# Modulation product of each DeltaNet head: from sixteen accumulating TensorE matmuls to partial products on GpSimd and four matmuls with ones

## The chip, the cores and the metric

The kernel runs on one core of a Trainium2 chip. The metric is the device time of one execution in microseconds (us), the median of several runs. A core has TensorE (matmuls, results in PSUM), VectorE, ScalarE and GpSimd (elementwise work), and SyncE, whose queue issues nearly all of the transfers here. The profiles call them PE (PEld for its weight loads), DVE, ACT, POOL and SP.

## What is computed

One layer of a hybrid backbone, over 512 latent and 128 context tokens of width 1024. What matters here is the modulation, and that DeltaNet runs head by head:

```python
m = jax.nn.silu(cond) @ w_ada + b_ada      # 1024 -> 6144, for cond = c and cond = c_ctx
sh1, sc1, g1, sh2, sc2, g2 = jnp.split(m, 6, axis=-1)
h = modulate(x, norm1_g, sh1, sc1)          # the first third of m is needed at once
qkv, z, bl, al, na, gt = split_in(h, w_in)
o_dn = deltanet_branch(...)                 # 8 heads, each with a triangular solve per chunk
x = x + g1 * merge(...)                     # the other two thirds are needed from here on
x = x + g2 * swiglu(modulate(x, norm2_g, sh2, sc2), ...)
```

## The kernel before

The first 2048 columns of `w_ada` are multiplied at the start. The other 4096 are spread over the eight DeltaNet heads, 512 columns a head in two halves of 256 (`PAIR`). A half of the weights, 8 row blocks of 128 x 256, is loaded into `WA`, one buffer for both halves: the queue of SyncE issues the first half in `opening` (L984), the second in `ada_second` (L988) once the first has been read. TensorE makes a half with `ada_rows` (L1285): eight matmuls, one for each row block k, with the two columns of `csT` (SiLU of the two conditions) as weights, spread over four column groups j = k % 4 of the array, so that four partial sums stand in rows 32j of bank 4. ScalarE copies them to `arow` ("ada half", L2265, and "ada rows", L2280), and `rows_out` (L993) stores them to rows 32j + 2h of `heads_rows`. In the last head, matmuls with a selecting matrix (L1656) add the four partial sums of all heads and turn them, and ScalarE copies them to `mods`.

The order on each engine is written out by hand. A `Steps` object counts the named steps of an engine, and others wait for a step's value. In a head TensorE interleaves two things. One is the DeltaNet head itself: block products P4, Y4, P5, Y5 (`wide`, L1553) and their turns (L1559), P6, Y6 (L1593, L1600), then a scan of five steps. The other is the dense projection of the next strips (L1311, six matmuls per step k), handed out by `filler(fill, n)`; the table `before` says how many steps stand in front of which block product, twelve in front of P4:

```python
for n in (4, 5):
    filler(fill, before[f"P{n}"])
    wait(dve_dn, f"X{n - 1}")
```

X3, which P4 waits for, is made by VectorE. Its chain begins with the ten products of L2909, goes on with transposes and shuffles (L2919 to L2931), then 15 pairs of "term" (L2945) and "lane" (L2947), each waiting for the one before it, and ends with L2954. Among them stand splits of the weights into a rounded part and a rest (`small`, L2903), `vrow` (L2936, L2937), and later the copies of P6 and Y6 (L2988, L2991).

GpSimd has three instructions in a head: the product "A" (L3569), which waits for X3 and which the scan needs, and the two sums of the decays (L3556, L3559).

Of the kernel before, what the change touches and what calls it, by code (L numbers as in the profile page):

```python
# [14 lines left out]
P = 128  # L15
# [98 lines left out]
def pe_steps():  # L114
    names = ["turn k v"]
    for n in (4, 5):
        names += [f"P{n} wide"] + (["ada half"] if n == 4 else []) + [f"P{n}", f"Y{n} wide"] + (["ada rows"] if n == 5 else []) + [f"Y{n}"]
    names += ["P6", "Y6"]
    for s in range(NT):
        if s:  # L120
            names += [f"ks {s} {d}" for d in "fb"]
        names += [f"y {s} {d}" for d in "fb"]
        names += [f"av {s} {d}" for d in "fb"]
    return names + ["norm", "kq", "turn o"]


def act_steps():
    names = ["kq", "L32", "L diag", "hi 1", "hi 2", "L pairs", "kd", "hi 2 late", "P4", "hi 3", "ada half", "Y4", "hi 4", "P5 wide", "P5", "Y5 wide", "Y5", "ada rows", "hi 5", "P6", "hi z", "decay", "Y6"]
# [140 lines left out]
POOL_STEPS = ["A", "dt"]  # L269
# [154 lines left out]
def build(nc, A):  # L424
    top = ExitStack()
    with top:
# [227 lines left out]
        sb("under_vrow", [P, 2 * 136 * U - 120 * U], dn)  # L654
        all_rows = sb("all_rows", [P, 120 * U], dn)[:, :]
# [8 lines left out]
        ob = sb("ob", [P, 2, NT, P], dn)  # L664
        prm = sb("prm", [P, NPRM, U], dn)
# [246 lines left out]
        def _(e):  # L912
# [59 lines left out]
            def opening(h, decays_of_next):  # L972
# [27 lines left out]
            def head(h, strips_after_next):  # L1000
# [12 lines left out]
                rows_out(h)  # L1013
# [9 lines left out]
                extra_store(h, 2)  # L1023

# [78 lines left out]
            rows_out(last)  # L1103
# [11 lines left out]
            pa_in(1)  # L1115
            e.wait_ge(st_e, 16 * (NE * (H - 1) + NE_LAST - 1) + 16)
# [139 lines left out]
        def _(e):  # L1256
# [202 lines left out]
            def head(h, part):  # L1459
# [58 lines left out]
                def filler(queue, n):  # L1518
# [9 lines left out]
                    "first": (12, 0, 3, 1, 1, 1, 1, 0, 2, 1, 1, 1),  # L1528
                    "mid": (12, 2, 2, 2, 2, 2, 2, 1, 3, 2, 1, 1),
# [9 lines left out]
                wait(act_dn, "silu v", h - 1)  # L1539
                for w in range(2):  # L1540
# [21 lines left out]
                for n in (4, 5):  # L1562
# [74 lines left out]

                def turn_o():
# [26 lines left out]
                if not more:  # L1665
# [366 lines left out]
        def _(e):  # L2032
# [167 lines left out]
            def head(h, part):  # L2200
# [4 lines left out]

                def big(at):
# [56 lines left out]
                wait(pe_dn, "ada half")  # L2263
                e.wait_ge(rows_kept, h * 4 * 16)
                act_dn.done(e.activation(arow[:, 0:2 * P], ps[:, 4, 0:2 * P], ACT.Copy), "ada half")  # L2265
# [13 lines left out]
                wait(pe_dn, "ada rows")  # L2279
                act_dn.done(e.activation(arow[:, 2 * P:4 * P], ps[:, 4, 0:2 * P], ACT.Copy), "ada rows")  # L2280
# [58 lines left out]
                if not more:  # L2339
                    e.wait_ge(ld_f0, 48)  # L2340
                    wait(pool_dn, "A")
                    act_na.done(e.activation(sq0, f0[:, 0:2, :], ACT.Square), "sq 0")
                    e.wait_ge(mods_mm, 1)
# [12 lines left out]
                if more:  # L2356
                    norm(h)
                    products_out(h + 1)
# [338 lines left out]
        def _(e):  # L2697
# [389 lines left out]
            e.wait_ge(pe_dn.sem, pe_dn.value(H - 1, "ada rows"))  # L3087
# [118 lines left out]
            e.wait_ge(mods_out, 1)  # L3206
# [329 lines left out]
        def _(e):  # L3536
# [12 lines left out]
            pool_dn.leave_out("dt")  # L3549
            pool_dn.settle(e)  # L3550
# [9 lines left out]

            def head(h, more):
                def wait(steps, name, turn=h):
                    e.wait_ge(steps.sem, steps.value(turn, name))

                wait(dve_dn, "X3")
# [8 lines left out]
                else:  # L3574
                    pool_dn.pass_to("A")

            for h in range(H - 1):
# [80 lines left out]
```

## Time and profile before

| | |
|---|---|
| median of 3 runs | 1302.97 us (1302.94 to 1303.77) |
| the profiled execution | 1302.37 us, its span 1300.6 us |
| TensorE busy | 1284.3 us, 99% |
| VectorE busy | 962.6 us, 74% |
| ScalarE busy | 701.2 us, 54% |
| GpSimd busy | 172.8 us, 13% |
| a middle head of DeltaNet | 74 us (282 to 356, for one) |

Busy is time in which an instruction of the engine runs. Matmuls overlap each other, so a busy TensorE need not be at its peak, and what an instruction costs there is read from the distance between starts. Times in the rows below count from the span's start.

### The profile page before, as it was taken

The numbers are of one execution on the slowest core, as the hardware profiler recorded it, in microseconds if no ns is written. First come the engines' busy times: TensorE is split into PE (matmuls) and PEld (weight loads), VectorE is DVE, ScalarE is ACT, GpSimd is POOL, SyncE is SP. The second block draws the span as 40 slices with busy tenths as digits, with TensorE's granted clock in tenths as the row PEclk, the third lists the DMA queues.
The fourth block names the chain that finished last, engine by engine and source line by source line (L and its number), as shares of the span: only waits on it lengthen the run. The fifth ranks groups of instructions, "written<-read, shape, count | busy, mean of one in ns | idle before, by whom it ended". The sixth has DMA issues, their size and how long they took to land.

```text
span 1300.6 us, 26090 instructions
## 1 busy us (share of the span) xinstructions
PE 1284.3 (99%) x9814; PEld 1212.4 (93%) x9814; DVE 962.6 (74%) x2396; ACT 701.2 (54%) x1578; POOL 172.8 (13%) x161
## 2 busy tenths in 40 slices
PE   7999999999999999999999999999999999999998
PEld 6898999999999999999988889999999999999998
DVE  6677867667686867767456666668999698987995
ACT  5564746465564746465366664347564355634643
POOL 1002020202001020200302320000103300041022
PEclk9999999999999999999999999999999999999999
DMA  9743543434243334325335216431323323233313
GB/s 313 242 131 96 166 122 100 118 94 118 55 142 90 116 103 120 89 72 153 115 113 169 77 51 207 124 82 33 98 67 97 98 70 93 66 100 96 83 57 106
DMA packets 207715, 144.51 MB, mean 111 GB/s; under 512 B 9455, under 2 KB 197015, under 8 KB 207463
## 3 DMA queue, kind: packets, MB, share of 16 engines
q1 hardware_dynamic: 207303, 142.72, 37.4%
q8 instruction: 78, 1.28, 0.4%
q14 instruction: 46, 0.38, 0.1%
q10 hardware_dynamic: 288, 0.13, 0.0%
HBM read 126.67 MB, written 17.99 MB: 111 GB/s over the span
## 4 chain that ended last, share of the span: by engine, by line
PE 92%; DVE 3%; SPq 2%; ACT 1%; issue 1%; DMA 1%; DVEq 0%; ACTq 0%
PE ps L1311 32%; PE ps L1957 25%; PE ps L1700 7%; PE ps L1615 3%; PE ps L1841 2%; PE ps L1937 2%; PE ps L1553 2%; PE ps L1622 2%; SPq L931 2%; PE ps L1439 1%; PE ps L1634 1%; PE ps L1809 1%; PE ps L1285 1%; PE ps L1795 1%; PE ps L1916 1%; PE ps L1693 1%
## 5 line engine op out<-in xcount | busy, mean ns | idle before, releaser
L1311 PE MATMUL ps<-hT_r,WAH_r 128*128 128x320 f32 x624 | 154.9, 329 | 0.5
L1311 PE MATMUL ps<-xT_r,WAH_r 128*128 128x320 f32 x624 | 142.0, 309 | 0.0
L1957 PE MATMUL ps<-d_part_r,W_r 128*128 128x320 f32 x660 | 136.7, 310 | 1.1 <-DVE xT L3388 0.7
L1311 PE MATMUL ps<-hT_r,W_r 128*128 128x320 f32 x588 | 132.6, 308 | 0.0
L1311 PEld LDWEIGHTS ps<-hT_r,WAH_r 128*128 128x128 f32 x624 | 100.3, 189 | 10.8 <-issue 9.8
L1957 PEld LDWEIGHTS ps<-d_part_r,W_r 128*128 128x128 f32 x660 | 107.5, 188 | 2.0 <-DVE xT L3388 1.3
L1957 PE MATMUL ps<-t_big_r,W_r 128*128 128x320 f32 x380 | 107.6, 311 | 0.7 <-ACT naT L2576 0.4
L1311 PEld LDWEIGHTS ps<-xT_r,WAH_r 128*128 128x128 f32 x624 | 104.5, 188 | 0.0
L1957 PE MATMUL ps<-b_part,W_r 128*128 128x320 f32 x456 | 101.2, 309 | 0.0
L1311 PEld LDWEIGHTS ps<-hT_r,W_r 128*128 128x128 f32 x588 | 97.9, 188 | 0.1
L1957 PE MATMUL ps<-t_small_r,W_r 128*128 128x320 f32 x304 | 93.9, 309 | 0.0
L1311 PE MATMUL ps<-hT_r,naT_r 128*128 128x320 f32 x398 | 90.9, 309 | 0.5 <-DVE xT_r L2753 0.4
L3569 POOL TENSOR_TENSOR gm<-sqkq,dt 128x1280 f32<-128x1280 f32 x8 | 23.5, 2938 | 500.6 <-DVE Xc L2954 500.6
L1957 PEld LDWEIGHTS ps<-b_part,W_r 128*128 128x128 f32 x456 | 76.2, 188 | 0.0
L3623 POOL TENSOR_TENSOR oT<-oT 128x512 f32<-128x512 f32 (+1 forms) x12 | 19.9, 1658 | 408.7 <-PE ps L1957 280.0
L1311 PE MATMUL ps<-hT_r,WH_more 128*128 128x320 f32 x286 | 70.8, 329 | 0.3
L1957 PEld LDWEIGHTS ps<-t_big_r,W_r 128*128 128x128 f32 x380 | 69.0, 188 | 2.1 <-ACT naT L2576 1.5
L1311 PEld LDWEIGHTS ps<-hT_r,naT_r 128*128 128x128 f32 x398 | 66.2, 188 | 4.0 <-DVE xT_r L2753 3.1
L3388 DVE SCALAR_TENSOR_TENSOR xT<-ps,mods,xT 128x192 f32<-128x192 f32 (+2 forms) x132 | 51.0, 421 | 20.5 <-PE ps L1957 19.9
L2518 ACT ACTIVATE W_r<-oT 128x512 fp32r<-128x512 f32 (+1 forms) x101 | 61.0, 607 | 7.3 <-PE ps L1957 7.3
L1311 PE MATMUL ps<-xT_r,WH_more 128*128 128x320 f32 x286 | 64.9, 308 | 0.0
L1957 PEld LDWEIGHTS ps<-t_small_r,W_r 128*128 128x128 f32 x304 | 57.1, 188 | 0.0
(489 smaller groups left out, 3426.7 us busy)
## 6 DMA issues: line engine op xcount, KB each, us to landing
oT<-in_ffn_w SPq DMA_DIRECT2D x44, 512.0 KB, 5.2
W<-in_w_in SPq DMA_DIRECT2D x36, 512.0 KB, 4.5
WAH<-in_w_ada SPq DMA_DIRECT2D x16, 1024.0 KB, 7.1
naT<-in_w_in SPq DMA_DIRECT2D x24, 512.0 KB, 4.2
ext_dram<-naT SPq DMA_DIRECT2D x28, 320.0 KB, 4.2
oT<-in_ffn_w SPq DMA_DIRECT2D x32, 256.0 KB, 3.9
tA<-ext_dram SPq DMA_DIRECT2D x16, 320.0 KB, 3.7
GCB<-gc_dram SPq DMA_DIRECT2D x7, 640.0 KB, 4.6
```

The costliest lines, as they stand in the source:

```text
L931: e.dma_start(WP[i][:, 4 * j:4 * j + 4, kind * PAIR:(kind + 1) * PAIR], src).then_inc(ld_wp[i][j], 16)
L1311: m = e.matmul(ps[:, bank + b, 0:n], w[:, k, :], x[:, k, a:a + n], start=k == 0 and i == 0, stop=k == KD - 1 and i == 2, skip_group_check= ...
L1553: m = e.matmul(ps[g:g + 32, 5, r:r + P], one[:, u, :], other[:, u, :], start=True, stop=True, skip_group_check=True)
L1615: m = e.matmul(ps[:, 2 + d, w * P:(w + 1) * P], kq[:, tile[d], w, :], S[:, d, :], start=True, stop=True, skip_group_check=True)
L1622: m = e.matmul(ps[:, (4, 6)[d], 0:P], XT[:, u, :], rr[:, d, :] if s else vrow[:, CT, :], start=True, stop=True)
L1700: m = e.matmul(ps[:, bank + b, 0:n], w[:, k, :], x[:, k, a:a + n], start=k == 0 and i == 0, stop=k == k_n - 1 and i == 2, skip_group_check ...
L1841: m = e.matmul(ps[:, PB_BANKS[n % 3] + b, 0:c], w, x[:, a:a + c], start=k == 0 and i == 0, stop=k == KP - 1 and i == 2, skip_group_check=True)
L1937: m = e.matmul(ps[:, UP_BANKS[p][s] + b, 0:HT], w[i][:, k % 4, :], operand(xp, k, b), start=k == 0 and n == 0, stop=k == KD - 1 and n == 2 ...
L1957: m = e.matmul(ps[:, bank, 0:HT], w[i][:, k, :], x[i][:, k, :], start=start and k == 0 and j == 0, stop=k == half - 1 and j == 2, skip_gro ...
L2518: act_ff.done(e.activation(w_big[i][:, 0:tiles_half(p), :], raw_half(p, s, j), ACT.Copy), f"{o} {p}")
L3388: m = e.scalar_tensor_tensor(x, ps[:, bank, a - half * HT:a - half * HT + w], mods[:, 2 * g + s + 40, c:c + 1], x, ALU.mult, ALU.add)
L3569: pool_dn.done(e.tensor_tensor(typed(AT[:, :, :]), kqs[:, :, 1, :].unsqueeze(1).to_broadcast([P, 2, NT, P]), typed(dtm[:, :, :]), ALU.mult ...
```

## The change

The eight row blocks of a half are no longer multiplied by TensorE. GpSimd scales each block with the two columns of `csT` (per row of the block, that is per partition) and adds up the eight results: 16 `tensor_scalar` of 128x256 and 7 `tensor_tensor` of 128x512 a half. The first half stands in front of "A", the second behind the decay sums. What is left is one sum over the 128 partitions for each condition and half. TensorE makes it at the head's end with four matmuls with ones, and ScalarE evacuates all with one copy. `WA` is free for the next load when GpSimd has read it. The stores to `heads_rows` are single rows now, at the end of the head's part of the queue; in the last head they stand behind the load of the second `w_pa` strip. In TensorE's order the filler steps of the gaps in which the halves stood are shared out anew; in the middle heads one moves from in front of P6 to in front of the turn of Y5.

```diff
-POOL_STEPS = ["A", "dt"]
+POOL_STEPS = ada_names(0) + ["A", "dt"] + ada_names(1)
...
-                e.wait_ge(pe_dn.sem, pe_dn.value(h - 1, "ada rows"))
+                e.wait_ge(pool_dn.sem, pool_dn.value(h - 1, "plus 1 7"))
                 e.dma_start(WA, w_ada[:, :, ds((16 + h * 4) * P, 2 * P)]).then_inc(ld_wa[0], 16)
...
-                e.wait_ge(pe_dn.sem, pe_dn.value(h, "ada half"))
+                e.wait_ge(pool_dn.sem, pool_dn.value(h, "plus 0 7"))
                 e.dma_start(WA, w_ada[:, :, ds((18 + h * 4) * P, 2 * P)]).then_inc(ld_wa[1], 16)
...
             def rows_out(h):
-                e.wait_ge(act_dn.sem, act_dn.value(h, "ada rows"))
+                e.wait_ge(mods_out, h + 1)
                 for j in range(4):
-                    e.dma_start(heads_rows[32 * j + 2 * h:32 * j + 2 * h + 2, :], arow[32 * j:32 * j + 2, :]).then_inc(rows_kept, 16)
+                    v, half = j // 2, j % 2
+                    row = 32 * half + 2 * h + v
+                    e.dma_start(heads_rows[row:row + 1, half * PAIR:(half + 1) * PAIR], arow[32 * j:32 * j + 1, 0:PAIR]).then_inc(rows_kept, 16)
...
-                    "first": (12, 0, 3, 1, 1, 1, 1, 0, 2, 1, 1, 1),
-                    "mid": (12, 2, 2, 2, 2, 2, 2, 1, 3, 2, 1, 1),
+                    "first": (12, 1, 2, 1, 1, 1, 1, 1, 1, 1, 1, 1),
+                    "mid": (12, 2, 2, 2, 2, 2, 2, 2, 2, 2, 1, 1),
...
-                    if n == 4:
-                        wait(act_dn, "kd")
-                        pe_dn.done(ada_rows(4, 2 * P, WA, ld_wa[0:1], h * 16 + 16), "ada half")
...
-                    if n == 5:
-                        wait(act_dn, "ada half")
-                        pe_dn.done(ada_rows(4, 2 * P, WA, ld_wa[1:2], h * 16 + 16), "ada rows")
...
+                def ada_of_head():
+
+                    wait(pool_dn, "plus 1 7")
+                    wait(act_dn, f"v {NT - 1} b")
+                    for j in range(4):
+                        m = e.matmul(ps[32 * j:32 * j + 32, 4, 0:PAIR], ONES[:, 0:32], ada_sums[:, j % 2, j // 2, :], start=True, stop=True, skip_group_check=True)
+                    m.then_inc(mods_mm, 1)
...
                         norm_rows()
+                        ada_of_head()
+                    if not more and k == 0:
+                        ada_of_head()
                     if not more and k == KD // 2:
                         e.wait_ge(rows_kept, H * 4 * 16)
...
+                def ada_rows_out():
+
+                    e.wait_ge(mods_mm, h + 1)
+                    if h:
+                        e.wait_ge(rows_kept, h * 4 * 16)
+                    e.activation(arow[:, 0:PAIR], ps[:, 4, 0:PAIR], ACT.Copy).then_inc(mods_out, 1)
...
+            def ada_half(h, half):
+
+                e.wait_ge(ld_wa[half], h * 16 + 16)
+                if h and not half:
+                    e.wait_ge(mods_mm, h)
+                total = ada_sums[:, half, :, :]
+
+                def times(k):
+
+                    out = ada_parts[:, k % 3, :, :] if k else total
+                    if k > 3:
+                        e.wait_ge(pool_dn.sem, pool_dn.value(h, f"plus {half} {k - 3}"))
+                    elif 0 < k and (h or half):
+                        e.wait_ge(pool_dn.sem, pool_dn.value(h - 1 + half, f"plus {1 - half} {(6, 7, 5)[k % 3]}"))
+                    for v in range(2):
+                        m = e.tensor_scalar(out[:, v, :], WA[:, k, :], csT[:, k, v:v + 1], None, ALU.mult)
+                    pool_dn.done(m, f"times {half} {k}")
+
+                times(0)
+                times(1)
+                for k in range(1, KD):
+                    if k + 1 < KD:
+                        times(k + 1)
+                    e.wait_ge(pool_dn.sem, pool_dn.value(h, f"plus {half} {k - 1}" if k > 1 else f"times {half} 1"))
+                    pool_dn.done(e.tensor_tensor(total, total, ada_parts[:, k % 3, :, :], ALU.add), f"plus {half} {k}")
...
             def head(h, more):
...
+                ada_half(h, 0)
                 wait(dve_dn, "X3")
...
+                ada_half(h, 1)
```

To make room, `all_rows`, the solve's shuffled rows, moves into `ob`, which is free then.

## Rows read from the trace of the kernel before

**Rows 1.** The page: busy time, TensorE's granted clock in 40 slices, last chain by engine.
```profile
PE 1284.3 (99%) x9814; PEld 1212.4 (93%) x9814; DVE 962.6 (74%) x2396; ACT 701.2 (54%) x1578; POOL 172.8 (13%) x161
...
PEclk9999999999999999999999999999999999999999
...
PE 92%; DVE 3%; SPq 2%; ACT 1%; issue 1%; DMA 1%; DVEq 0%; ACTq 0%
```
**Rows 2.** Timeline, TensorE, 312 to 324: start, duration, line, instructions.
```profile
312.33 0.74 PE L1553 MATMUL ps<-tri,Xc 128*32 128x128 f32 x18
...
313.98 0.57 PE L1311 MATMUL ps<-hT_r,WAH_r 128*128 128x320 f32 x2
...
322.85 0.85 PE L1553 MATMUL ps<-tri,Xc 128*32 128x128 f32 x20
323.63 0.56 PE L1311 MATMUL ps<-hT_r,WH_more 128*128 128x320 f32 x2
```
**Rows 3.** What ended TensorE's idle time before L1553: us in all, times.
```profile
  DVE Xc L2954: 1.4, 7
```
**Rows 4.** Timeline, VectorE, 292 to 313.
```profile
292.57 2.71 DVE L2909 SCALAR_TENSOR_TENSOR tri<-sqkq,bk,dt 128x128 f32<-128x128 f32 x10
...
300.25 1.21 DVE L2903 TENSOR_TENSOR naT_r<-naT,WAH_r 128x1024 fp32r<-128x1024 f32 x1
301.38 0.68 DVE L2936 TENSOR_TENSOR vrow<-ps,nrm 128x512 f32<-128x512 f32 x1
...
302.24 0.31 DVE L2945 TENSOR_TENSOR P6c<-P6c,all_rows 128x150 f32<-128x150 f32 x1
...
311.65 0.49 DVE L2954 TENSOR_TENSOR Xc<-P6c,lv_c 128x320 f32<-128x320 f32 x1
```
**Rows 5.** Groups of instructions, GpSimd, by shape: busy us, mean ns, idle before.
```profile
L3626 POOL TENSOR_TENSOR naT<-oT 128x512 f32<-128x512 f32 x9 | 12.0, 1330 | 2.4 <-PE ps L1957 1.5 <-POOL oT L3623 0.4
...
L3626 POOL TENSOR_TENSOR naT<-oT 128x384 f32<-128x384 f32 x3 | 3.0, 1012 | 0.4
...
L3541 POOL MEMSET X<- 128x320 f32 x1 | 0.4, 366 | 0.0
```
**Rows 6.** Timeline of the feed-forward part, VectorE and GpSimd, 883 to 1001.
```profile
883.91 0.49 DVE L3312 TENSOR_TENSOR b_part<-t_big,b_part 128x320 fp32r<-128x320 f32 x1 [0.33 <-ACT d_part_r L2564]
883.99 1.56 POOL L3623 TENSOR_TENSOR oT<-oT 128x512 f32<-128x512 f32 x1 [128.64 <-DMA oT<-in_ffn_w]
884.32 1.58 DVE L3312 TENSOR_TENSOR d_part_r<-t_big,d_part_r 128x320 fp32r<-128x320 f32 x1
...
997.15 0.68 DVE L3246 TENSOR_TENSOR W_r<-oT,W_r 128x512 fp32r<-128x512 f32 x1
997.47 2.12 POOL L3623 TENSOR_TENSOR oT<-oT 128x512 f32<-128x512 f32 x1 [3.52 <-PE ps L1957]
997.75 0.68 DVE L3246 TENSOR_TENSOR oT_r<-oT,W_r 128x512 fp32r<-128x512 f32 x1
...
999.74 1.30 POOL L3626 TENSOR_TENSOR naT<-oT 128x512 f32<-128x512 f32 x1
1000.86 0.55 DVE L3388 SCALAR_TENSOR_TENSOR xT<-ps,mods,xT 128x320 f32<-128x320 f32 x1 [1.08 <-PE ps L1957]
```
**Rows 7.** The first half's load in the window 282 to 290: issue and landing.
```profile
L984 SPq DMA_DIRECT2D WAH<-in_w_ada x1: 581/581/581, 282.8 to 282.8; - x1
...
DMA to landing us min/median/max: 8.7/8.7/8.7
```
**Rows 8.** Timeline, 320 to 337: GpSimd, VectorE, TensorE.
```profile
320.54 2.94 POOL L3559 TENSOR_TENSOR dt<-dt,msk 128x1280 f32<-128x1280 f32 x1
...
334.53 0.48 DVE L2988 COPY P6c<-ps 64x320 f32<-64x320 f32 x1
...
336.05 0.80 PE L1600 MATMUL ps<-XT,P6c 64*64 64x64 f32 x20
```
**Rows 9.** Timeline, SyncE's queue, 625 to 640: the last head's row stores.
```profile
634.79 2.45 SPq L993 DMA_DIRECT2D heads_rows<-arow  x4
```
**Rows 10.** Transfers by line: count, KB each, median us from issue to landing.
```profile
S<-in_state_dn SPq DMA_DIRECT2D x16, 64.0 KB, 1.9
```

More of the change, by code:

```diff
@@ L116, in pe_steps @@
     for n in (4, 5):
-        names += [f"P{n} wide"] + (["ada half"] if n == 4 else []) + [f"P{n}", f"Y{n} wide"] + (["ada rows"] if n == 5 else []) + [f"Y{n}"]
+        names += [f"P{n} wide", f"P{n}", f"Y{n} wide", f"Y{n}"]
     names += ["P6", "Y6"]
@@ L127, in act_steps @@
 def act_steps():
-    names = ["kq", "L32", "L diag", "hi 1", "hi 2", "L pairs", "kd", "hi 2 late", "P4", "hi 3", "ada half", "Y4", "hi 4", "P5 wide", "P5", "Y5 wide", "Y5", "ada rows", "hi 5", "P6", "hi z", "decay", "Y6"]
+    names = ["kq", "L32", "L diag", "hi 1", "hi 2", "L pairs", "kd", "hi 2 late", "P4", "hi 3", "Y4", "hi 4", "P5 wide", "P5", "Y5 wide", "Y5", "hi 5", "P6", "hi z", "decay", "Y6"]
     for s in range(NT):
@@ L266, in dve_na_steps, with ada_names @@
     return names
-POOL_STEPS = ["A", "dt"]
+def ada_names(half):
+    names = [f"times {half} 0", f"times {half} 1"]
+    for k in range(1, KD):
+        names += [f"times {half} {k + 1}"] if k + 1 < KD else []
+        names += [f"plus {half} {k}"]
+    return names
+POOL_STEPS = ada_names(0) + ["A", "dt"] + ada_names(1)
 OPERANDS = ("A11", "S1", "S2", "A12", "S3", "S4", "A22")
@@ L653, in build @@
         sqkq = sb("sqkq", [P, NT, 2, P], dn)
-        sb("under_vrow", [P, 2 * 136 * U - 120 * U], dn)
-        all_rows = sb("all_rows", [P, 120 * U], dn)[:, :]
+        ada_sums = sb("ada_sums", [P, 2, 2, PAIR], dn)
+        ada_parts = sb("ada_parts", [P, 3, 2, PAIR], dn)
+        sb("under_vrow", [P, 2 * 136 * U - 10 * PAIR], dn)
         vrow = sb("vrow", [P, NT, P], dn)
@@ L664, in build @@
         ob = sb("ob", [P, 2, NT, P], dn)
+        all_rows = ob[:, :, :, :].rearrange("p a t c -> p (a t c)")[:, 0:120 * U]
         prm = sb("prm", [P, NPRM, U], dn)
@@ L1012, in head @@
                 extra_store(h, 1)
-                rows_out(h)
                 if strips_after_next:
@@ L1023, in head @@
                 extra_store(h, 2)
+                rows_out(h)
             e.wait_ge(rows_zero, 1)
@@ L1102, in _ @@
             extra_store(last, 4)
-            rows_out(last)
             e.wait_ge(pe_dn.sem, pe_dn.value(last, "Y6"))
@@ L1115, in _ @@
             pa_in(1)
+            rows_out(last)
             e.wait_ge(st_e, 16 * (NE * (H - 1) + NE_LAST - 1) + 16)
@@ L1539, in head @@
                 wait(act_dn, "silu v", h - 1)
+                if h:
+                    e.wait_ge(mods_out, h)
                 for w in range(2):
@@ L1673, in head @@
                         pe_na.done(m, f"sums {'qk'[j]} 0")
+                    e.wait_ge(mods_out, H)
                     for j in range(2):
@@ L2262, in head @@
                 big("3")
-                wait(pe_dn, "ada half")
-                e.wait_ge(rows_kept, h * 4 * 16)
-                act_dn.done(e.activation(arow[:, 0:2 * P], ps[:, 4, 0:2 * P], ACT.Copy), "ada half")
                 if part != "first":
@@ L2278, in head @@
                 act_dn.done(e.activation(Yc[:, :, :], ps[:, 6, 0:U * 32].rearrange("p (u c) -> p u c", u=U), ACT.Copy), "Y5")
-                wait(pe_dn, "ada rows")
-                act_dn.done(e.activation(arow[:, 2 * P:4 * P], ps[:, 4, 0:2 * P], ACT.Copy), "ada rows")
                 big("5")
@@ L2357, in head @@
                     norm(h)
+                    ada_rows_out()
                     products_out(h + 1)
@@ L3086, in _ @@
             e.wait_ge(gain_q, 1)
-            e.wait_ge(pe_dn.sem, pe_dn.value(H - 1, "ada rows"))
+            e.wait_ge(pool_dn.sem, pool_dn.value(H - 1, "plus 1 7"))
             scaled_q(0, ss0)
@@ L3549, in _ @@
             pool_dn.leave_out("dt")
+            pool_dn.pass_to("times 0 0")
             pool_dn.settle(e)
@@ L3559, in decays @@
                 pool_dn.done(e.tensor_tensor(typed(dt[:, :, :]), typed(dt[:, :, :]), upto, ALU.add), "dt")
+            def ada_half(h, half):
[14 more added lines that the diff above has]
+                times(1)
+                for k in range(1, KD):
+                    if k + 1 < KD:
+                        times(k + 1)
+                    e.wait_ge(pool_dn.sem, pool_dn.value(h, f"plus {half} {k - 1}" if k > 1 else f"times {half} 1"))
+                    pool_dn.done(e.tensor_tensor(total, total, ada_parts[:, k % 3, :, :], ALU.add), f"plus {half} {k}")
             def head(h, more):
@@ L3574, in head @@
                 else:
-                    pool_dn.pass_to("A")
+                    pool_dn.leave_out("dt")
+                ada_half(h, 1)
+            e.wait_ge(cond_silu, 1)
             for h in range(H - 1):
```

6 lines of the change are left out of this document (4 added, 2 removed).

## Prediction

> **What bounds the kernel now.** I read the page first. TensorE is busy in 99% of the span and makes up 92% of the chain that ended last; its clock digit is 9 in every slice [rows 1]. So what leaves TensorE is gained, as long as nothing else makes it wait. The second view was TensorE's timeline in a middle head of DeltaNet, around the two places where the modulation product stands. After the block product P4 (L1553) TensorE runs the half product (L1285) before the next dense matmul (L1311); after P5 it goes straight on [rows 2]. The third view was what TensorE waits for at L1553: in seven of the eight heads it stands 0.2 us for VectorE's L2954, the instruction that makes X3 [rows 3]. That small wait matters most: TensorE has used up its twelve filler steps just as VectorE ends its solve. There is no slack in front of P4, and a VectorE that comes later by d makes TensorE stand still for d. The fourth view was VectorE's own timeline in that stretch. From L2909 at 292.57 to the end of L2954 at 312.14 it has hardly a gap [rows 4]; 30 small products and sums (L2945, L2947) fill most of the time from 302.24 on, each waiting for the one before.
>
> **What the change takes from TensorE.** From P4's start to the next dense matmul 1.65 us pass with the half product in between, 0.78 us at P5 without it [rows 2]. So a half costs 0.87 us, two halves in eight heads 13.9 us. Added at each head's end are four matmuls of the size of the eight that make a half: half of 0.87 is 0.44 us, and I take 0.5 with the switch in front, 4.0 us in all (bounds 3.5 and 6). The filler steps moved between the gaps are the same number. The two evacuations on ScalarE become one; it sits idle around both places, and I price them at nothing.
>
> **What it gives GpSimd.** Each half is 16 scaled copies of 128x256 and seven sums of 128x512. A sum of 128x512 takes 1.33 us in its group (1.30 undisturbed) and one of 128x384 takes 1.01 [rows 5, 6]. The trace has no GpSimd instruction with one tensor and a scalar. Below it lies a memset of 320 elements, 0.37 us, above it a two-input sum of 256 elements, which the two sizes give as 1.33 - 0.32 = about 0.70 us [rows 5]. One input and one output is nearer to the memset; I take 0.35 (bounds 0.31 and 0.70). A half is then 16 x 0.35 + 7 x 1.30 = 14.7 us. The Trainium skill (GPSIMD Engine Reference, Engine selection) calls one-input elementwise work roughly line-rate and two-input work about twice as slow as VectorE; by that the copy would be near 0.3 us and this forecast some 4 us smaller. Two halves are 29.4 us of a head of 74 us, in which GpSimd has had three instructions of 2 to 3 us, so it is not itself the bound.
>
> **When it runs.** The first half's weights are issued at 282.77 and land 8.7 us later, at 291.5 [rows 7]. GpSimd starts there and works through 14.7 us of its own time, just over VectorE's solve, which begins at 292.57.
>
> **What that costs VectorE.** The two engines get in each other's way, and the trace shows it. At 884.32 VectorE starts L3312, otherwise 0.49 us, while GpSimd runs a sum from 883.99 to 885.55: it takes 1.58 us, that is it is held for about 1.1 us, until 0.13 us before GpSimd ends [rows 6]. It goes the other way too: GpSimd's sum at 997.47 takes 2.12 in place of 1.30 us because two VectorE instructions without a wait between them run first. VectorE's L3388, which takes one tensor from PSUM, keeps its normal 0.55 us beside GpSimd [rows 6]. The held ones have both tensors in SBUF. In before's DeltaNet stage GpSimd's three instructions happen to stand beside transposes and such, so nobody is held.
>
> In the solve, L2909, L2903, L2945, L2947 and L2954 have both tensors in SBUF. I walk through one head. Until 292.6 GpSimd does 1.1 of its 14.7 us. L2909 waits for the rest of one instruction, 0.3, then holds GpSimd for 2.7 us. From 295.3 to 300.25 VectorE mostly transposes and shuffles with one input; GpSimd gets 5.0 us done and, with the copies and L2923, delays VectorE by 0.8. L2903 waits 0.5, and beside L2936 and its neighbour, which read PSUM, GpSimd does 0.95. So it has 14.7 - 1.1 - 0.3 - 5.8 - 0.5 - 0.95 = 6.05 us left when the chain of 30 starts. There they take turns. Two copies and a sum are 2.0 us: the sum holds VectorE 1.1 us as above, a copy, mostly hidden in VectorE's own gaps, 0.15. Three such turns make 4.2 us. VectorE is late by 0.3 + 0.8 + 0.5 + 4.2 = 5.8 us at L2954, and TensorE waits as long. Heads 0 and 7 have the load at slightly other times; I count them alike: 8 x 5.8 = 46.4 us. If the copies cost 0.70, a half is 20.3 us, the 5.6 more fall into the chain, copies hold 0.5 each, and the delay is 1.6 + 11.65 x 2.1 / 2.7 = 10.7 us per head, 39 more. If VectorE's chain keeps GpSimd out although it waits between its instructions, only the 1.6 us are left, 33.6 less.
>
> **The second half** starts when GpSimd ends the decay sums, 323.5 [rows 8], and lasts to about 340. VectorE has idle time there, but a weight split (L2903) stands in front of the copy L2988 at 334.53, which TensorE's Y6 at 336.05 waits for [rows 8], and one filler step fewer now stands in front of P6. I take 0.7 us per head, 5.6 in all (bounds 0 and 12).
>
> **The end of the last head.** Before, the row stores left at 634.79 [rows 9], long before the last strip. Now they can leave only after the four matmuls at the last strip's step 0, and TensorE wants them four steps, about 3.5 us, later. They need 0.5 (matmuls), 0.6 (evacuation), 2.45 (the four issues) and a landing; small state loads land in 1.9 us [rows 10]. That is 5.5 us: a stall of about 2 us, once (bounds 0 and 5).
>
> **The sum.** -13.9 + 4.0 + 46.4 + 5.6 + 2.0 = +44.1 us. The profiled execution took 1302.37 us (span 1300.6 and 1.8 around it), 0.6 under the median of 1302.97, so the forecast is 1302.4 + 44.1 = 1346.5 us, 3.4% slower.
>
> **Rivals.**
> (a) Faster. GpSimd's work does not reach the chain in front of P4: its instructions wait, not VectorE's, and they have until the scan, behind Y6, to finish. Then -13.9 + 4.0 + 2.0 = -7.9, 1294.5 us. It decides if VectorE's delay per head stays under (13.9 - 4.0 - 2.0) / 8 = 1.0 us. For it speaks that GpSimd was also held in the trace; against it that L3312 was held 1.10 us by a single sum [rows 6], and seven of them stand in a half.
> (b) VectorE keeps the port in its chain but pays around it: 1.6 us per head. -13.9 + 4.0 + 12.8 + 5.6 + 2.0 = +10.5, 1313 us. Against it: a wait between two instructions leaves a gap, and GpSimd's instruction is already pending.
> (c) The clock falls. In before TensorE never pauses in the heads for more than a few tenths of a us and is granted full speed throughout [rows 1]. A pause of 5.8 us in each head is new. If behind each one TensorE runs at 1.2 GHz for as long as it paused, it loses half of 5.8 us, 2.9 per head: 1346.5 + 23 = 1369.5 us. No row here prices it. The Trainium skill (TensorE: Matmul & The Clock Gate, Rules for kernel authors) warns that idle gaps between bursts of matmuls bring the clock back to the lower level; by that this rival would hold.
>
> **Chances.** The forecast as worked out 0.70, with its own range 1318 to 1380 from the bounds of the copy and of the chain; (a) 0.12; (b) 0.08; (c) 0.10. A range of 1306 to 1375 leaves out (a) and the far end of the slow copies, together under 0.2. A measurement of this kernel tells 0.2%, 2.6 us, from nothing. Faster by more than that is (a), 0.12; within it lies the low end of (b), 0.03; slower 0.85.
>
> **What would show it.** In the changed profile VectorE's L2945 and L2947 should show a maximum well over their 0.31 us; TensorE's wait at the block product for VectorE should grow from 0.2 to about 5.8 us per head; GpSimd should be busy some 240 us more, with sums over 1.30 us where they were held. TensorE has 96 matmuls fewer. If instead L2954 keeps its distance of 19.6 us from L2909, the held chain was wrong and (a) holds; if the copies take 0.7 us, the forecast is too low; if PEclk shows digits under 9 behind P4, (c) holds.

## The result and the profile after

The changed kernel takes 1369.91 us (median of 4 runs, 1365.24 to 1372.98); the kernel before, on the same chip, 1303.37 us (4 runs). The ratio is 1.0507, 95% interval 1.0476 to 1.0538: slower by 66.5 us. The forecast was 1346.5 us, range 1306 to 1375. The profiled execution is the slowest of the four, 1372.98 us with a span of 1371.2.

The page of the kernel after:

```profile
PE 1295.0 (94%) x9622; PEld 1220.7 (89%) x9622; DVE 1044.4 (76%) x2396; ACT 698.8 (51%) x1570; POOL 589.7 (43%) x529
...
PEclk9999999999999999999999999999999999999999
...
PE 73%; DVE 19%; issue 3%; SPq 2%; ACT 1%; DMA 1%; DVEq 0%; ACTq 0%
...
L3602 POOL TENSOR_SCALAR ada_parts<-WAH,csT 128x256 f32<-128x256 f32 x224 | 236.2, 1066 | 0.0
...
L3611 POOL TENSOR_TENSOR ada_sums<-ada_sums,ada_parts 128x512 f32<-128x512 f32 x112 | 151.6, 1353 | 1.3
```

Against [rows 1], TensorE's share falls from 99% to 94% as the program got longer, and VectorE now makes up 19% of the chain that ended last. GpSimd has two new groups with 422 us together with the 32 copies that write `ada_sums` directly; the forecast had some 240. TensorE has 192 records fewer, two for each of the 96 matmuls.

The lines of those groups, and VectorE's products in the chain of 30 (minimum, median and maximum in ns):

```profile
L3602 POOL TENSOR_SCALAR ada_parts<-WAH,csT x224: 915/927/1956, 83.1 to 698.5; 128x256 f32<-128x256 f32 x112
...
L3611 POOL TENSOR_TENSOR ada_sums<-ada_sums,ada_parts x112: 1257/1287/2252, 86.7 to 700.8; 128x512 f32<-128x512 f32 x112
...
L2970 DVE TENSOR_TENSOR P6c<-P6c,ob x120: 175/266/1442, 89.9 to 673.0; 128x150 f32<-128x150 f32 x8, 128x140 f32<-128x140 f32 x8, 128x130 f32<-128x130 f32 x8, 128x120 f32<-128x120 f32 x8
```

A scaled copy of 128x256 takes 0.92 us. That is over the 0.35 us that I took and over my upper bound of 0.70 us. A half is thus 16 x 0.92 + 7 x 1.29 = 23.7 us of GpSimd's time and not 14.7, and in the heads the first half takes 26 us from its first copy to its last sum, because its own instructions are held too (a sum by up to 1 us, 2.25 in all). A sum is as long as forecast. The longest product in VectorE's chain went to 1.44 us.

How the two engines stand against each other, in the timeline of head 2, VectorE first and then GpSimd:

```profile
247.67 1.44 DVE L2970 TENSOR_TENSOR P6c<-P6c,ob 128x150 f32<-128x150 f32 x1
249.14 0.47 DVE L2972 TENSOR_TENSOR P6c<-P6c 128x150 f32<-128x150 f32 x1
249.65 0.31 DVE L2970 TENSOR_TENSOR P6c<-P6c,ob 128x140 f32<-128x140 f32 x1
249.99 0.52 DVE L2972 TENSOR_TENSOR P6c<-P6c 128x140 f32<-128x140 f32 x1
250.54 0.29 DVE L2970 TENSOR_TENSOR P6c<-P6c,ob 128x130 f32<-128x130 f32 x1
250.87 1.35 DVE L2972 TENSOR_TENSOR P6c<-P6c 128x130 f32<-128x130 f32 x1
```
```profile
247.65 1.29 POOL L3611 TENSOR_TENSOR ada_sums<-ada_sums,ada_parts 128x512 f32<-128x512 f32 x1
248.91 1.89 POOL L3602 TENSOR_SCALAR ada_parts<-WAH,csT 128x256 f32<-128x256 f32 x2
250.78 1.30 POOL L3611 TENSOR_TENSOR ada_sums<-ada_sums,ada_parts 128x512 f32<-128x512 f32 x1
```

Each of these sums holds the VectorE instruction that meets it: it ends only 0.17 and 0.15 us after the sum's own end (0.04 to 0.18 over all heads) and takes 1.44 and 1.35 us in place of 0.3. So a sum that an instruction meets near its start costs VectorE 1.1 us (0.92 to 1.14). Beside the copies VectorE's instructions go on; some of them are longer, by 0.07 to 0.25 us.

Ahead of the chain the sums also hold VectorE's instructions with a single input. In head 1 the copy L2940 takes 1.21 us, 0.24 before, beside this sum:

```profile
159.96 1.21 DVE L2940 COPY P6c<-lv_c 128x160 f32<-128x160 f32 x1
```
```profile
159.73 1.35 POOL L3611 TENSOR_TENSOR ada_sums<-ada_sums,ada_parts 128x512 f32<-128x512 f32 x1
```

The shuffles (L2956) that run beside sums keep their length to 0.01 us.

VectorE's solve (start of the ten products, L2909 before and L2934 now, to the end of X3, L2954 before and L2979 now) took 19.57 us in heads 1 to 7 and 20.40 in head 0. It now takes 28.77, 26.49, 26.98, 26.82, 26.51, 27.44, 26.52 and 27.57 us, 59.7 us more in all. In heads 1 to 6 the rise ahead of the chain of 30 is 1.2 to 2.0 us; in the chain itself, 9.90 us before, it is 5.3 us in four of them and 6.2 in two.

Where TensorE waits for it, in the timeline of head 2 and in the list of waits (us in all, times, longest):

```profile
247.03 0.53 PE L1324 MATMUL ps<-hT_r,WH_more 128*128 128x320 f32 x2 [1.33 <-DVE naT_r L2928]
...
253.85 0.46 PE L1324 MATMUL ps<-hT_r,naT_r 128*128 128x320 f32 x2
257.39 0.53 PE L1324 MATMUL ps<-hT_r,WAH_r 128*128 128x320 f32 x2 [3.09 <-DVE P6c L2970]
...
260.69 0.46 PE L1324 MATMUL ps<-hT_r,W_r 128*128 128x320 f32 x2
263.80 0.85 PE L1568 MATMUL ps<-tri,Xc 128*32 128x128 f32 x20 [2.65 <-DVE Xc L2979]
```
```profile
PE ps L1568 <- DVE Xc L2979: 16.9, 8, 2.7
PE ps L1324 <- DVE P6c L2970: 15.1, 6, 3.1
PE ps L1324 <- DVE naT_r L2928: 8.7, 5, 2.1
```

There are three pauses in each solve of heads 1 to 6, in head 2 1.33, 3.09 and 2.65 us, together 7.1. Only the last stands at the block product; over the eight heads it makes up 16.9 us of 51.4. At the first a dense matmul waits for the weight split (L2928) in front of the chain. At the second it waits for the split that is queued on VectorE inside the chain: that split ends at 257.25, and the product that the profile names stands behind it.

Windows right behind the first matmuls after P4 in heads 3, 4 and 6, and behind the end of the last head (the columns are the length, then the busy time of PE, PEld, DVE, ACT and POOL with their instructions, the granted clock as a share of 2.4 GHz, the DMA engines' share and GB/s):

```profile
345.20:348.60 3.40, 3.40 (x30) 2.95 (x23) 1.62 (x4) 1.44 (x2) 2.57 (x1) 0.58 0.33 113
427.10:430.60 3.50, 3.50 (x30) 3.04 (x31) 1.91 (x4) 1.44 (x2) 2.86 (x1) 0.59 0.43 147
591.00:594.40 3.40, 3.40 (x30) 2.95 (x23) 1.70 (x4) 1.44 (x2) 2.66 (x1) 0.58 0.37 127
730.90:737.80 6.90, 6.90 (x28) 6.87 (x29) 1.02 (x2) 4.54 (x14) 0.00 (x0) 0.54 0.00 0
```

The page's digits (tenths of a slice) hide it, but in these stretches TensorE is granted 1.2 GHz most of the time. From P4 to the next head's ten products 54.15 us pass in heads 1, 2 and 5, and 55.5 to 55.6 in heads 3, 4 and 6: 1.4 us each. The end of the last head:

```profile
729.95 1.55 PE L1676 MATMUL ps<-lv_c,heads_rows 128*128 128x16 f32 x8 [1.72 <-DMA heads_rows<-arow]
731.34 0.88 PE L1324 MATMUL ps<-hT_r,WAH_r 128*128 128x320 f32 x2
732.02 0.73 PE L1324 MATMUL ps<-xT_r,WAH_r 128*128 128x320 f32 x2
```

TensorE waits 1.7 us for the rows' load, as forecast (2), and behind it pairs of dense matmuls take 0.73 us in place of 0.46. From the last X3 to the end 697.3 us pass, 692.7 before: 4.6 more. The profile lists one more fall that matters, from 71.6 to 75.0 us, just ahead of head 0's solve.

### The profile page after: what moved, and what is told of

The parts are those of the page before. It is cut to its first block, busy times and chain, and to the rows that moved or that the text cites. A ratio compares the mean times of both kernels' runs of the same rounds, so it can differ in the third digit from the quotient of the medians.

```text
span 1371.2 us, 26065 instructions
## 1 busy us (share of the span) xinstructions
PE 1295.0 (94%) x9622; PEld 1220.7 (89%) x9622; DVE 1044.4 (76%) x2396; ACT 698.8 (51%) x1570; POOL 589.7 (43%) x529
## 4 chain that ended last, share of the span: by engine, by line
PE 73%; DVE 19%; issue 3%; SPq 2%; ACT 1%; DMA 1%; DVEq 0%; ACTq 0%
PE ps L1978 24%; PE ps L1324 19%; PE ps L1721 7%; DVE P6c L2972 4%; DVE P6c L2970 3%; PE ps L1862 2%; PE ps L1624 2%; PE ps L1958 2%; DVE tri L2934 2%; PE ps L1631 2%; SPq L942 2%; PE ps L1568 1%; DVE ob L2956 1%; PE ps L1643 1%; PE ps L1452 1%
## 5 line engine op out<-in xcount | busy, mean ns | idle before, releaser
L3602 POOL TENSOR_SCALAR ada_parts<-WAH,csT 128x256 f32<-128x256 f32 x224 | 236.2, 1066 | 0.0
L1324 PE MATMUL ps<-hT_r,WAH_r 128*128 128x320 f32 x624 | 158.9, 336 | 22.8 <-DVE P6c L2970 10.6
L3611 POOL TENSOR_TENSOR ada_sums<-ada_sums,ada_parts 128x512 f32<-128x512 f32 x112 | 151.6, 1353 | 1.3
L1324 PE MATMUL ps<-xT_r,WAH_r 128*128 128x320 f32 x624 | 145.3, 315 | 0.0
L1324 PEld LDWEIGHTS ps<-hT_r,WAH_r 128*128 128x128 f32 x624 | 103.2, 194 | 33.3 <-issue 24.5
L1324 PEld LDWEIGHTS ps<-xT_r,WAH_r 128*128 128x128 f32 x624 | 107.6, 193 | 0.0
L3602 POOL TENSOR_SCALAR ada_sums<-WAH,csT 128x256 f32<-128x256 f32 x32 | 34.6, 1092 | 152.1 <-DMA WAH<-in_w_ada 152.1
L1978 PEld LDWEIGHTS ps<-b_part,W_r 128*128 128x128 f32 x456 | 76.2, 188 | 0.0
L3654 POOL TENSOR_TENSOR tri<-tri 128x128 f32<-128x128 f32 x80 | 36.6, 496 | 82.8 <-DMA tri<-rpb_table_dram 82.0
L2276 ACT ACTIVATE zs<-ps 128x384 f32<-128x384 f32 x32 | 15.7, 492 | 101.9 <-PE ps L1568 101.7
```

What stands on the lines that cost most here:

```text
L1324: m = e.matmul(ps[:, bank + b, 0:n], w[:, k, :], x[:, k, a:a + n], start=k == 0 and i == 0, stop=k == KD - 1 and i == 2, skip_group_check= ...
L1978: m = e.matmul(ps[:, bank, 0:HT], w[i][:, k, :], x[i][:, k, :], start=start and k == 0 and j == 0, stop=k == half - 1 and j == 2, skip_gro ...
L3602: m = e.tensor_scalar(out[:, v, :], WA[:, k, :], csT[:, k, v:v + 1], None, ALU.mult)
L3611: pool_dn.done(e.tensor_tensor(total, total, ada_parts[:, k % 3, :, :], ALU.add), f"plus {half} {k}")
L3654: m = e.tensor_tensor(dst, b[:, rel + j, :, :], w[:, rel + j, :].unsqueeze(1).to_broadcast([P, ROWS, KC]), ALU.add)
```

## Experiments

All are timed against the kernel before on the same chip: 1303.95 us beside no_work, half0, half1 and no_sums, 1303.62 beside no_copies, added, dummies and vector_half, 1303.65 beside dummies_short and vector_tuned. The first five set two tuples that say which of a half's eight blocks are scaled and which are added; behind no_work the cuts show that line against no_work's.

**no_work: the new structure without the work.** Of each half only the two copies of the first row block are left, 4 of a head's 46 instructions.

```diff
+            COPIED, SUMMED = ((0,), (0,)), ((), ())
```

> The changed kernel with only the first row block of each half scaled on GpSimd: 14 copies and 7 sums of each half are left out, loads, waits, stores and TensorE's four matmuls stay (the modulation rows are incomplete). Theory (GpSimd's reads hold VectorE in the solve, and TensorE waits): the solve from the ten products to X3 is back at 19.6 us a head, and the time is 1302 - 13.9 + 4.8 for the new matmuls + 2 to 5 for the stall at the last head's end: 1295 to 1299 us. Rival (the loss comes from what else moved: the rows of the solve now in ob, the later stores, the waits): the solve stays near 27 us and the time above 1340 us.

1298.15 us (4 runs), ratio 0.9956, interval 0.9941 to 0.9971. The solve is back at 19.57 us; in heads 1 to 6 53.0 us pass from P4 to the next head, 1.15 fewer than before. So taking the halves off TensorE and adding four matmuls saves 1.15 us in such a head. In head 0 it saves nothing, 47.43 us against 47.41. With next to no work on GpSimd the change gains 5.8 us. The whole loss, 66.5 + 5.8 = 72 us, is GpSimd's work.

**half0 and half1: one half's work alone.**

```diff
-            COPIED, SUMMED = ((0,), (0,)), ((), ())
+            COPIED, SUMMED = (range(KD), (0,)), (range(1, KD), ())   # half0
+            COPIED, SUMMED = ((0,), range(KD)), ((), range(1, KD))   # half1
```

> As the changed kernel, with the first half's product whole and only the first row block of the second half. Theory: all of the loss in the solve stays (about 7.4 us a head), the 1.2 us a head behind P4 go: 1370 - 10 = about 1360 us. Rival (the second half's late end delays the scan and the next load, and that is the larger part): under 1335 us.

> As the changed kernel, with the second half's product whole and only the first row block of the first half. Theory: the solve is back at 19.6 us, 1.2 us a head remain for conv pieces and copies held in the scan: 1297 + 10 = about 1307 us. Rival: over 1335 us.

half0: 1361.76 us (1354.34 to 1364.01, 4 runs), ratio 1.0433 (1.0401 to 1.0465). Its solve takes 27.1 us in heads 1 to 7, and the rest of the head stays at 53.0. half1: 1305.67 us (10 runs), ratio 1.0017 (1.0008 to 1.0026). Its solve is untouched at 19.56 us, no VectorE product in the chain is over its normal length:

```profile
L2970 DVE TENSOR_TENSOR P6c<-P6c,ob x120: 175/234/320, 87.0 to 608.7; 128x150 f32<-128x150 f32 x8, 128x140 f32<-128x140 f32 x8, 128x130 f32<-128x130 f32 x8, 128x120 f32<-128x120 f32 x8
```

From P4 to the next head it takes 54.2 us, 1.15 more than no_work, and in head 0 48.4, 1.0 more. Over no_work the first half costs 63.6 us and the second 7.5, together 71.1 of the 72. Place decides. The same instructions cost eight times as much beside the solve as behind it. (The four runs of half0 lie 10 us apart, so the 63.6 is good to some us only.)

**no_sums and no_copies: which instructions hold VectorE.** Copies alone; then all sums with only the copies of blocks 0 to 3.

```diff
-            COPIED, SUMMED = ((0,), (0,)), ((), ())
+            COPIED, SUMMED = (range(KD), range(KD)), ((), ())        # no_sums
+            COPIED, SUMMED = ((0, 1, 2, 3), (0, 1, 2, 3)), (range(1, KD), range(1, KD))   # no_copies
```

> All 16 copies of each half, none of the seven sums (the product is that of one row block). Theory (a sum reads two tensors from SBUF and holds VectorE for 1.1 us; a copy takes 0.9 us but holds it for 0.2 or less): the solve is 21 to 22 us long, the time 1305 to 1320 us. Rival (GpSimd holds VectorE for as long as any instruction of its reads, whatever it is): 14.6 us of copies leave the solve at 25 us or more, the time over 1340 us.

> All seven sums of each half, and of the 16 copies only the eight for row blocks 0 to 3 (later sums add a part again). Theory (each sum holds VectorE for 1.1 us, a copy for about 0.13): the sums follow each other closely and five to seven of them fall on the solve, which is 25 to 27 us long; about 1350 us. Rival (sums and copies cost by their own duration): 16.4 us of GpSimd time a half in place of 23.6 makes the loss in the solve 5.1 us a head, 24.7 us and 1335 us or less.

no_sums: 1310.67 us (4 runs), ratio 1.0049 (1.0032 to 1.0066). no_copies: 1351.27 us (4 runs), ratio 1.0366 (1.0352 to 1.038). The chain's products in the one and in the other:

```profile
L2970 DVE TENSOR_TENSOR P6c<-P6c,ob x120: 175/234/331, 89.2 to 616.6; 128x150 f32<-128x150 f32 x8, 128x140 f32<-128x140 f32 x8, 128x130 f32<-128x130 f32 x8, 128x120 f32<-128x120 f32 x8
```
```profile
L2970 DVE TENSOR_TENSOR P6c<-P6c,ob x120: 175/234/1397, 89.6 to 655.4; 128x150 f32<-128x150 f32 x8, 128x140 f32<-128x140 f32 x8, 128x130 f32<-128x130 f32 x8, 128x120 f32<-128x120 f32 x8
```

What the copies do lengthen is the other instruction of a pair, here in no_sums (0.317 us at most before):

```profile
L2972 DVE TENSOR_TENSOR P6c<-P6c x120: 177/242/574, 89.5 to 616.8; 128x150 f32<-128x150 f32 x8, 128x140 f32<-128x140 f32 x8, 128x130 f32<-128x130 f32 x8, 128x120 f32<-128x120 f32 x8
```

With 256 copies of 0.92 us and not one sum, the longest product is 0.33 us, the longest instruction of the other kind 0.57 us (0.28 at most over its normal length), and the solve takes 21.2 us (+1.7). With the sums and half the copies the longest product is 1.40 us and the solve takes 25.2 us (+5.6). A copy is longer on GpSimd than expected and yet costs VectorE little; a sum is what holds it.

**added: the work without the change.** The kernel before keeps its product on TensorE, and GpSimd does all copies and sums beside it, read by nobody.

```diff
             def head(h, more):
...
+                ada_half(h, 0)
                 wait(dve_dn, "X3")
...
+                ada_half(h, 1)
```

> The kernel before with TensorE's product left as it is, and GpSimd's copies and sums of both halves added beside it into buffers that nobody reads (the solve's rows in ob, and the loads wait for both readers). Theory: the solve is 26 to 28 us long as in the changed kernel, and the price of GpSimd's work alone shows: 1370 + 13.9 - 4.8 - 5 (no stall at the end) = about 1374 us. Rival (the loss is tied to TensorE's new order of fillers and the waits for the head's end): under 1350 us.

1370.14 us (4 runs), ratio 1.0512 (1.0496 to 1.0528), solve 26.8 us in heads 1 to 7. GpSimd's work alone costs 66.5 us and gives the solve of the changed kernel to 0.1 us. Neither the new order of TensorE nor the new waits are needed to explain the loss in the solve. It is 66.5 us here and not 72 for two reasons. Nothing happens at the end (from the last X3 692.3 us pass, 697.3 in the changed kernel). And the second half costs less beside the old order: from P4 to the next head 54.55 us pass in heads 1, 4, 5 and 6, 0.4 more than before, where half1 has 1.15 over no_work.

**dummies and dummies_short: what the clock costs.** In every head but head 0, matmuls that nobody reads fill the second and the third of the three pauses, so that the clock should not fall. The first pause stays open.

```diff
+                def keep_busy(n):
+                    for _ in range(n):
+                        e.matmul(ps[:, 7, 0:P], sq_c[:, ONE, :], sq_c[:, ONE, :], start=True, stop=True, skip_group_check=True)
...
                         if kind == order[2]:
+                            keep_busy(20)      # dummies_short: 12
...
+                    if n == 4 and part != "first":
+                        keep_busy(18)          # dummies_short: 8
```

> The changed kernel whole, with 38 more matmuls a head on constants (from the second head on) in the two places where TensorE stands for VectorE in front of P4; their results are not used. They should last as long as the pause, 20 x 0.142 and 18 x 0.142 us, and keep the clock up. Theory (the drops to half speed that the profile lists, one a head, cost something, 1.4 us where they fall behind P4): the drops in the heads vanish and the time falls by 4 to 10 us, to 1360 to 1366. Rival (the pause alone sets the time, the drops are hidden in it): unchanged at 1370, or above it if the matmuls are too long.

> The changed kernel with dummy matmuls on the constant ones in the two pauses of each head behind the first, now 12 ahead of the third strip's wait for the residual and 8 ahead of the wait for X3. In the run with 20 and 18 of them one took 0.22 us (40 records in 4.4 us), so that they lasted 4.4 and 4.0 us against pauses of 3.1 and 2.7 us, and the five-term products began 2.1 to 5.2 us behind X3's end; 12 and 8 last 2.6 and 1.8 us and should lie inside the pauses. Theory (the granted clock that fell behind the pauses cost some 8 to 14 us of the change's 66): 1356 to 1364 us, no half-speed stretch in heads 1 to 7, and P4 within 1 us behind X3's end. Rival (the pauses themselves are the whole price, the clock's fall was hidden under the next wait): 1368 to 1373 us with the clock at 1.00. If the clock still falls, the run tells nothing on this and I shall say so.

dummies: 1387.95 us (4 runs), ratio 1.0657 (1.0637 to 1.0676), 18 us more than the changed kernel. Its timeline in head 2:

```profile
252.95 4.62 PE L1486 MATMUL ps<-sq_c 128*128 128x128 f32 x40
257.33 0.54 PE L1324 MATMUL ps<-hT_r,WAH_r 128*128 128x320 f32 x2
...
260.93 4.18 PE L1486 MATMUL ps<-sq_c 128*128 128x128 f32 x36
265.04 0.85 PE L1575 MATMUL ps<-tri,Xc 128*32 128x128 f32 x20
```

My size was off: one takes 0.22 us, so the two blocks last 4.4 and 4.0 us where the pauses were 3.1 and 2.7, and P4 begins at 265.04 with X3 ready since 261.66. In heads 1 to 7 P4 comes 2.1 to 5.2 us behind X3, 26 us together. That run priced the dummies, not the clock.

dummies_short: 1366.54 us (1364.45 to 1369.01, 4 runs), ratio 1.0479 (1.0464 to 1.0494). It lies between its two expectations, and the clock still fell in some solves (in head 2, from 250 to 253 us, pairs of dense matmuls took 0.74 us), so the total alone settles nothing. These falls begin 11 to 13 us into the solves of heads 1, 2, 5 and 6, right behind the first pause, which lasts 1.8 to 3.0 us there. The places do. Windows behind P4 in heads 3 and 4 (same columns as above):

```profile
346.50:349.90 3.40, 3.40 (x39) 3.20 (x40) 2.22 (x5) 1.44 (x2) 2.92 (x1) 1.00 0.94 302
427.80:431.20 3.40, 3.40 (x39) 3.19 (x40) 2.23 (x5) 1.44 (x2) 2.95 (x1) 1.00 0.43 149
```

The clock is at 2.4 GHz there, and from P4 to the next head 54.1 to 54.2 us pass in each of heads 1 to 6, never 55.5. So the fall behind P4 costs 1.4 us where it happens, three times in the changed kernel's profiled run, 4.2 us. What the clock costs in an average run is not shown, only estimated. The run of dummies_short with a mean clock of 0.999 took 1364.45 us, 5.5 less than the changed kernel's median; but it has waits of its own (P4 stands 1.2 us behind X3 in heads 5 and 6), and runs of one kernel differ by as much. The places in the changed kernel's profiled run, its slowest, give 4.2 us behind P4, about 3 at the end and about 1.4 ahead of head 0, together 9. So the clock is worth some 5 to 9 us, an estimate, and not 23.

**vector_half and vector_tuned: the second half on VectorE.** half1 shows that work behind the solve is cheap, and VectorE can scale and add in one instruction. The first half stays on TensorE. The second is 16 such instructions in VectorE's gaps behind X4, and four matmuls of 128 columns at the head's end. vector_tuned mends what vector_half's trace showed.

```diff
+                        out = ada_sums[:, v, :]
+                        if k:
+                            m = e.scalar_tensor_tensor(out, WA[:, k, :], csT[:, k, v:v + 1], out, ALU.mult, ALU.add)
...
-AT_GAPS = (6, 4, 3, 2, 1, 0, 0)
+AT_GAPS = (6, 2, 3, 2, 1, 1, 1)      # vector_tuned
...
-                    "first": (12, 0, 3, 1, 1, 1, 1, 1, 1, 1, 1, 1),
+                    "first": (12, 0, 3, 1, 1, 1, 1, 1, 3, 1, 0, 0),      # vector_tuned
...
-                    if not more and k == KD // 2:
+                    if not more and k == KD - 2:      # vector_tuned
```

> The kernel before with half 0 on TensorE as it was, and half 1 as 16 scale-and-add instructions on VectorE, spread over its own waits behind the solve (6 in front of Y5's copies, 4 in front of Y6's, 6 in the scan); GpSimd does nothing new, four matmuls of 128 columns close the half at the head's end. Theory (what leaves TensorE is gained if nobody is held in front of it): -7.0 + 8 x 0.35 = -4 us, and +2 to +5 for the stall at the last head's end: 1299 to 1304 us. Rival (VectorE has no room, its later copies make TensorE wait): 1306 us or more.

> The version with the second half on VectorE, mended where its trace lost time: in the first head PE waited 3.2 us for X64 (VectorE had six of the products ahead of it) and the clock fell behind it, together some 5 us, so two pieces of the first head's filler are moved ahead of that product; one product fewer before XT's copy in each head; and at the tail the select of the per-head rows stands two chunks later and its copy behind the last norm (0.9 us of wait for the rows' load). It saves one half's matmuls (0.87 us a head) for four matmuls with ones (0.34 us a head). Theory: 1301 to 1305 us, level with the kernel before or up to 0.2% faster. Rival (the VectorE products in the scan's gaps make the scan late by as much as the matmuls saved, and the first head still stalls): 1306 to 1310 us.

vector_half: 1309.61 us (5 runs), ratio 1.0039 (1.0025 to 1.0053), slower. The solve is untouched (19.56 us), but the interval from X3 to the next head's X3 falls by 0.08 us only, and the first one is 72.55 us against 67.48. There six of the new instructions stand on VectorE in front of the copies that make X64 (L3034). TensorE's timeline:

```profile
115.58 1.33 PE L1603 MATMUL ps<-X,tri 64*64 64x64 f32 x20 [3.19 <-DVE X L3034]
116.85 0.90 PE L1322 MATMUL ps<-hT_r,WAH_r 128*128 128x320 f32 x2
117.55 0.73 PE L1322 MATMUL ps<-xT_r,WAH_r 128*128 128x320 f32 x2
```

A wait of 3.2 us, and 1.2 GHz behind it. vector_tuned: 1302.42 us (1300.75 to 1302.94, 11 runs), ratio 0.9986 (0.9977 to 0.9995). The first interval is 69.39 us, the others 73.4 against 73.9. It is the fastest of the versions that compute everything, ahead of the kernel before by 0.14%. The interval just leaves out 1, but 0.14% is under the 0.2% that the prediction called the least that can be told, so this is no gain to count on. Its instructions:

```profile
L3009 DVE SCALAR_TENSOR_TENSOR ada_sums<-WAH,csT,ada_sums x112: 467/476/820, 113.1 to 656.2; 128x256 f32<-128x256 f32 x112
...
L3011 DVE TENSOR_SCALAR ada_sums<-WAH,csT x16: 345/350/354, 112.6 to 624.3; 128x256 f32<-128x256 f32 x16
```

A half is 14 x 0.48 + 2 x 0.35 = 7.4 us of VectorE, where GpSimd takes 23.7.

## Why the prediction came out as it did

The sign and the mechanism were right; several terms were too small. The time lies 23 us over the forecast, inside the range and near its upper end. In spans, 1300.6 to 1371.2, the 70.6 us are made of these:

| term | forecast | measured |
|---|---|---|
| halves off TensorE, four matmuls on | -13.9 + 4.0 = -9.9 | -7.0 in heads 1 to 6, 0 in head 0 (no_work) |
| VectorE late in the solve | +46.4 | +59.7 |
| second half behind the solve | +5.6 | 6.9 in heads 1 to 6, 1.0 in head 0 = +7.9 (half1) |
| X3 to P4 shorter (0.19 to 0.06 us; head 0: 0.51 to 0.06) | none | -1.4 |
| head 0's solve starts later; rest of its way to head 1 | none | +2.2, +0.2 |
| clock behind P4, three heads | a rival | +4.2 |
| from the last X3 to the end, head 7's halves with it | +2.0 | +4.6 |

The measured column sums to 70.4. The profiled execution is 3.1 us over the median, so the medians' 66.5 us hold less of some terms, of the clock's most likely.

**TensorE's saving.** In heads 1 to 6 1.15 us a head were saved, 1.24 forecast. In head 0 nothing was: in no_work TensorE waits 1.39 us there for VectorE's X64 at the block product L1602, where it waited 0.16 before. The forecast took it that what leaves TensorE is gained in all eight heads. Head 7's part can't be told from the tail.

**The length of a copy.** This step failed. I chose the memset as the nearer row because a scaled copy has one tensor in and one out, and took 0.35 us within 0.31 and 0.70. It takes 0.92 us, more than a two-input sum of the same size by the two sizes in [rows 5]. The trace of before had no such instruction, and neither end of a bound from other kinds of instruction held it. (The upper one is written as 1.33 - 0.32; the 0.70 comes from taking off 0.32 twice.) The Trainium skill (GPSIMD Engine Reference, Engine selection) calls one-input work on GpSimd roughly line-rate. The runs do not agree: VectorE scales the same 128x256 block in 0.35 us, 2.6 times faster.

**The hold on VectorE.** For a sum [rows 6] gave 1.1 us and the trace after shows 1.1. For a copy 0.15 was taken and 0.07 to 0.25 seen, though it lasts 0.92. So the working had a copy too short and its hold nearly right, and the upper branch (0.70 us a copy, 0.5 us held each, 10.7 us a head) had both ends wrong in opposite directions. What the longer copies do is to spread the seven sums out, so that more of them fall into the chain. The forecast had 6.05 us of GpSimd's work left when the chain starts, three turns; in head 2 13.1 us are left (247.67 to 260.80). Five sums hold the chain's instructions in heads 2 and 5, four in heads 1, 3, 4 and 6. At 1.1 us that is 5.5 and 4.4 of the 6.2 and 5.3 measured, the copies are the rest; 4.2 was forecast. Ahead of the chain the 1.6 us of the forecast stand against 1.2 to 2.0, but that is in part luck: the working let the one-input instructions there go nearly free, and the largest single delay in heads 1 to 6 is a sum that holds one of them (L2938, L2940 or L2946) for 0.5 to 1.0 us. The Trainium skill (SBUF — State Buffer, Who interferes with whom) says that an instruction of VectorE with two inputs in SBUF contends with a GpSimd instruction that reads SBUF, and calls the pair of ports that they share an exclusive lock. For the sums the trace agrees, 1.44 and 1.35 us; for the copies, which read SBUF too, it does not: they last 0.92 us and lengthen such an instruction by 0.28 at most.

**The place of the wait.** The forecast put all of it at the block product. In head 2 it is 2.65 us there, 3.09 us in the filler at the split that VectorE does inside the chain, and 1.33 us at the split in front of it. The total, 7.1 us, is near the 7.4 by which the solve is longer, since what is not waited at the one is waited at the other.

**The second half.** 0.7 us a head taken, 1.15 measured, inside the bounds of 0 to 12 in all. It is 0.4 in added, so a part of it belongs to TensorE's new order. Which VectorE instruction it holds was not isolated.

**The tail.** The stall is near the forecast (1.7 us for 2); the fall of the clock behind it, about 3 us by pairs of 0.73 us in place of 0.46, was in no term.

**The rivals.** (a), GpSimd waits and not VectorE, and (b), VectorE keeps its chain free, fall with the solve's 26.9 us and with added. (c) holds in kind and not in size. It assumed 1.2 GHz for as long as TensorE had paused, in each head, 23 us. The clock did fall behind pauses, but cost 1.4 us in some heads. In half0's profiled run the mean clock was 0.989 and still 53.0 us passed from P4 to the next head in every one of heads 1 to 6: there the slow stretches lay inside the solve, and what they lengthen is taken off the next pause. The forecast of (c), 1369.5 us, agrees with the measured time by chance: 13 us of the difference are VectorE's, 3 TensorE's smaller saving, 2 the second half's. The rule that the prediction cites for (c) stands in the Trainium skill (TensorE: Matmul & The Clock Gate) under the heading Why this matters for your kernels, not under the one that the prediction names; by it gaps bring the clock down, and in heads 3, 4 and 6, with windows at 0.58, the trace agrees. In head 2 the clock stayed up behind pauses of 3.09 and 2.65 us.

**The range.** The prediction gives 1318 to 1380 us as the forecast's own range from its bounds. Its working gives 39 more and 33.6 less, 1313 to 1385.5. The stated range of 1306 to 1375 doesn't hang on it.

**Head 0's late start.** no_work has 0.8 of the 2.2 us. The rest goes with the clock: in the five profiled runs of the new structure without a fall at 70 to 75 us the solve of head 0 starts at 76.2 to 77.3 us, and in the four with GpSimd's work and such a fall, the changed kernel's among them, at 78.4 to 79.0.

What stays open: what the clock costs in an average run, and how that divides between heads; why a sum holds VectorE for nearly all of its length and a copy does not.

## What to carry to other kernels

Work given to an idle engine is not free when it shares something with a busy one. Look for what stands beside the new instructions in time, not for the engine's busy share: the same half cost 63.6 us beside a chain of small two-input VectorE instructions and 7.5 us behind it. Where the trace has no row for an instruction, a bound from rows of other kinds is no bound; move the choice to a place where even a price twice as high is hidden. And if a chain has no slack, price each engine that touches the same memory during it per instruction that it holds, not per microsecond.

## What the runs showed of the hardware

- GpSimd scales a 128x256 block in 0.92 us and adds two of 128x512 in 1.29 us. VectorE scales the same block in 0.35 us, and scales and adds it in 0.48.
- A GpSimd sum holds a VectorE instruction with two inputs in SBUF, which ends only 0.04 to 0.18 us after the sum (1.44 us for one of 0.3); a GpSimd copy with a scalar lengthens such an instruction by 0.28 us at most. A sum holds VectorE's copies with one input too (1.21 us for one of 0.24), but not its shuffles (0.01 us).
- TensorE ran behind pauses of 1.8 to 3.1 us at 1.2 GHz in some heads and at 2.4 in others (head 2 of the changed kernel, behind 3.09 and 2.65 us); the mean clock changed from run to run (0.984 to 0.999 for the kernels with pauses). A fall behind P4 cost 1.4 us; one inside the solve cost nothing that shows.
